# First pair of tile 1's heads scored in the mixer, and the expert stage's schedule moved up by one step

## What is computed

```
q      = x1 @ w_q                                # 8 heads x 2 halves x 128
scores = einsum('bshcd,hcnd->bshcn', q, sub_keys)
s1, i1 = top_k(scores[..., 0, :], 16); s2, i2 = top_k(scores[..., 1, :], 16)
cand   = s1[..., :, None] + s2[..., None, :]     # 256 sums
top_s, pos = top_k(cand, 16);  ids = expert numbers at pos;  gates = softmax(top_s)
act    = gelu(einsum('td,tkd->tk', x1, u_tab[ids])) * gates
out    = layer_norm(alpha * x1 + einsum('tk,tkd->td', act, v_tab[ids]))
```

## Time and profile before

| what | value |
|---|---|
| median of three runs | 3395.33 us |
| profiled run | 3388.38 us, span 3386.7 us |
| TensorE (PE) busy | 2825.3 us, 83% |
| VectorE (DVE) busy | 1882.9 us, 56% |
| ScalarE (ACT) busy | 604.3 us, 18% |
| GpSimd (POOL) busy | 1479.7 us, 44% |
| mean granted TensorE clock | 0.914 |
| moved by DMA | 981.57 MB, mean 290 GB/s |

### The profile page before, as it was taken

One profiled execution on the slowest core, in us unless ns is written; L12 is line 12 of the kernel. 1 busy time (PEld: TensorE's weight loads), 2 busy tenths in 40 slices (PEclk: granted clock), 3 DMA queues, 4 the chain that ended last, 5 costly groups with the idle time before them and its releaser, 6 DMA issues.

```text
span 3386.7 us, 32687 instructions
## 1 busy us (share of the span) xinstructions
PE 2825.3 (83%) x10195; PEld 1391.7 (41%) x10195; DVE 1882.9 (56%) x4610; ACT 604.3 (18%) x1334; POOL 1479.7 (44%) x1348
## 2 busy tenths in 40 slices
PE   8999978666345888748779999999999999999995
PEld 3455544433112455524334444444444444444341
DVE  2334434787579788768855556546656544444013
ACT  1321123222001788700000000000000000000000
POOL 0011001343544344344465666566665556664452
PEclk9999979877667899778889999999999999999998
DMA  3100021455588899898899999999999999998995
GB/s 105 50 25 25 25 73 66 140 168 172 192 303 291 322 387 379 321 386 334 308 385 388 404 399 404 373 396 399 404 404 374 370 396 406 392 396 341 364 329 195
DMA packets 307579, 981.57 MB, mean 290 GB/s; under 512 B 29905, under 2 KB 57681, under 8 KB 306641
## 3 DMA queue, kind: packets, MB, share of 16 engines
q0 software_dynamic: 184320, 671.17, 52.2%
q1 hardware_dynamic: 120464, 307.85, 24.1%
q10 hardware_dynamic: 2624, 0.46, 0.1%
HBM read 941.63 MB, written 37.75 MB: 289 GB/s over the span
## 4 chain that ended last, share of the span: by engine, by line
PE 27%; issue 13%; POOL 12%; DMA 11%; DVE 5%; ACT 2%; ACTq 1%; DVEq 1%; another core or an unknown queue 0%; POOLq 0%
DMA v_ring<-in_peer_v_dram,ids_t 10%; PE part L1720 8%; PE hid L1701 8%; POOL u_ring L1639 7%; PE acc L1758 6%; POOL v_ring L1653 5%; PE turn_ps L1693 4%; DVE u_ring L2009 2%; ACT dense_sums L1798 1%; PE part L1729 1%; DMA u_ring<-in_peer_u_dram,ids_u 1%; ACTq L1799 1%; ACT dense_sums L1800 1%; ACT room L1846 0%; PE sc_ps L1772 0%
## 5 line engine op out<-in xcount | busy, mean ns | idle before, releaser
L2009 DVE CUSTOM_DVE_ANT_0 u_ring<-u_ring,x_rows_in 128x1024 f32<-128x1024 f32 x560 | 676.1, 1224 | 505.4 <-DMA u_ring<-in_peer_u_dram,ids_u 460.4
L1653 POOL DMA_INDIRECT v_ring<-in_peer_v_dram,ids_t x600 | 634.5, 1057 | 543.0 <-PE acc L1758 373.9
L1639 POOL DMA_INDIRECT u_ring<-in_peer_u_dram,ids_u x560 | 622.4, 1112 | 488.0 <-DVE dots L2009 335.5
L1720 PE MATMUL part<-room 128*128 128x512 f32 x1536 | 693.8, 602 | 80.4 <-DVE room L1989 73.5
L1701 PE MATMUL hid<-x1t_dense,room 128*128 128x384 f32 x2048 | 702.7, 497 | 5.3 <-DMA room<-in_peer_ut_dram 3.8
L1701 PEld LDWEIGHTS hid<-x1t_dense,room 128*128 128x128 f32 x2048 | 387.4, 193 | 341.1 <-issue 103.9
L1720 PEld LDWEIGHTS part<-room 128*128 128x128 f32 x1536 | 292.1, 193 | 441.5 <-issue 336.7
L1758 PE MATMUL acc<-v_ring,line 128*32 128x512 f32 x2400 | 315.0, 645 | 86.3 <-DMA v_ring<-in_peer_v_dram,ids_t 81.9
L1836 ACT ACTIVATE room<-hid 128x384 f32<-128x384 f32 x128 | 62.8, 491 | 1476.7 <-PE hid L1701 1173.1
L1999 DVE TENSOR_TENSOR dense_sums<-dense_sums,part 128x512 f32<-128x512 f32 x186 | 125.5, 684 | 292.9 <-PE part L1720 256.0
L411 PE MATMUL bank<-w_ring,xt 128*128 128x512 f32 x512 | 225.1, 592 | 2.6 <-issue 2.6
(11 more groups left out here) (315 smaller groups left out, 2605.6 us busy)
## 6 DMA issues: line engine op xcount, KB each, us to landing
wq_pair<-in_peer_wq_dram SPq DMA_DIRECT2D x32, 2048.0 KB, 8.8
room<-in_peer_ut_dram SPq DMA_DIRECT2D x128, 512.0 KB
room<-in_peer_v_dram SPq DMA_DIRECT2D x128, 512.0 KB
gate_grid<-room SPq DMA_DIRECT2D x6, 4096.0 KB, 13.3
room<-gate_grid SPq DMA_DIRECT2D x32, 768.0 KB
w_ring<-in_w_in_dram SPq DMA_DIRECT2D x5, 2048.0 KB, 8.0
v_ring<-in_peer_v_dram,ids_t POOLq DMA_INDIRECT x600
u_ring<-in_peer_u_dram,ids_u POOLq DMA_INDIRECT x560
```

Of the source, the lines that this page charges most:

```text
L1639: pool.indirect_dma_start(u_ring[:, n % U_RING, :], None, peer_u, bass.IndirectOffsetOnAxis(ap=ids_u[:, q, k:k + 1], axis=0))\
L1653: pool.indirect_dma_start(row, None, peer_v, bass.IndirectOffsetOnAxis(ap=ids_t[:, q % 2, token:token + 1], axis=0))\
L1720: last = mm.matmul(part[k % 3][:], weights[:, n % 2, i, d * P:(d + 1) * P], vd[:, slot, half * 512:(half + 1) * 512], start=(i == 0), stop ...
L2009: vec.tensor_tensor_reduce(u_ring[:, n % U_RING, :], u_ring[:, n % U_RING, :], x1[:, q % 2, :], 1.0, 0.0, ALU.mult, ALU.add, dots[:, q % 2 ...
```

## The change

After tile 0's four pairs the mixer makes a fifth choice-like pass (`NEXT_TILE`, at n = 35): tile 1's x1 is read back from DRAM into `x1t_first`, pair 0's weights are loaded, TensorE makes the queries and scores of tile 1's first pair, and ScalarE copies them to `sc_pair`; VectorE doesn't choose them there. SP then loads pair 1's weights. The last tile's projection waits for that copy. `sc_pair` and `q_pair` lie in a new buffer `y_rows`, which both stages share (the scan's `ys` and `sq` and the expert stage's `y` lie in it too).

In the expert stage tile 1's pair 0 then belongs to step −1: VectorE chooses it in step 0 from `sc_pair`, and TensorE starts with pair 1. All tables but tile 0's own starts (`U_AT[0]`, `V_AT[0]`) move up by one step, and tile 0's 32 quads go through ten steps instead of eleven, the last three with four quads. `STEPS` falls by one.

```diff
-        ys = sb("ys", [P, SSD], to=scan)
-        sq = sb("sq", [P, SSD], to=scan)
+        ys, sq, sc_pair = y_rows[:, 0:SSD], y_rows[:, SSD:2 * SSD], y_rows[:, 0:2 * DKEY]
...
-        q_pair = sb("q_pair", [P, 2 * DKEY])
+        q_pair = y_rows[:, 2 * DKEY:4 * DKEY]
...
+        NEXT_TILE = HEADS // 2 + 1
+        CHOICES = (*range(HEADS // 2), NEXT_TILE)
...
-            return g if rest == 0 and 0 <= g < HEADS // 2 else None
+            return g if rest == 0 and g in CHOICES else None
...
+                    if t == NT - 1:
+                        sp.wait_ge(wq_free, 1).then_inc(wq_free, -1)
+                        load_pair(1)
...
                     if t == NT - 3:
                         sp.wait_ge(wq_free, 1).then_inc(wq_free, -1)
-                        sp.dma_start(wq_pair[:], peer_wq[:, 0:2 * DKEY].rearrange("(c p) n -> p c n", p=P)).then_inc(wq_in, 16)
-                        sp.dma_start(keys_pair[:], keys_t[:, 0:2 * DKEY]).then_inc(wq_in, 16)
+                        sp.dma_start(x1t_first[:].rearrange("p c n -> p (c n)"), x1t_dram[P:2 * P, :]).then_inc(wq_in, 16)
+                        load_pair(0)
...
-                        pe.wait_ge(wq_in, 32).then_inc(wq_in, -32)
+                        landed = 48 if choice(n, 0) == NEXT_TILE else 32
+                        pe.wait_ge(wq_in, landed).then_inc(wq_in, -landed)
...
-                        act.sem_inc(pair_for_dve, 2)
+                        if choice(n, 2) != NEXT_TILE:
+                            act.sem_inc(pair_for_dve, 2)
...
-                        if (g := choice(n, 5 + which)) is not None:
+                        if (g := choice(n, 5 + which)) is not None and g != NEXT_TILE:
...
-CHOSEN_AT = {1: 0, 2: 4, 3: 8, 4: 12, 5: 20, 6: 40, 7: 72}
+CHOSEN_AT = {1: -1, 2: 3, 3: 7, 4: 11, 5: 19, 6: 39, 7: 71}
...
-DENSE_AT = 18
+DENSE_AT = 17
...
-U_AT = (0, 17, 34, 67, 100)
+U_AT = (0, 16, 33, 66, 99)
...
-V_COUNTS = ((2,) + 10 * (3,), (2,) + 30 * (1,), (2,) + 30 * (1,), (2,) + 30 * (1,), 16 * (2,))
-V_AT = (6, 34, 67, 100, 133)
+V_COUNTS = ((2,) + 6 * (3,) + 3 * (4,), (2,) + 30 * (1,), (2,) + 30 * (1,), (2,) + 30 * (1,), 16 * (2,))
+V_AT = (6, 33, 66, 99, 132)
...
-NORM_AT = (26, 65, 98, 131, 149)
+NORM_AT = (25, 64, 97, 130, 148)
...
-                sp.wait_ge(q_done, n)
+                sp.wait_ge(q_done, n - 1)
...
-                sp.wait_ge(sc_done, n)
+                sp.wait_ge(sc_done, n - 1)
...
-                    dve.wait_ge(sc_done, n + 1)
-                    best_eight(vec, dve, b, sc_ps).then_inc(sc_seen, 1)
+                    if n:
+                        dve.wait_ge(sc_done, n)
+                    best_eight(vec, dve, b, sc_ps if n else sc_pair).then_inc(sc_seen, 1)
```

More of the change, by code:

```diff
@@ L123, in build_mixer @@
                 d_skip, ssd_norm_g, ln1_g, ln1_b, x1_dram, x1t_dram, peer_wq, keys_t, peer_u,
-                ids_first, top_first, dots_first, wq_pair, keys_pair, kept):
+                ids_first, top_first, dots_first, wq_pair, keys_pair, y_rows, kept):
     vec, act_, mm = nc.vector, nc.scalar, nc.tensor
@@ L730, in build_mixer @@
         x1_first = sb("x1_first", [P, D])
-        q_pair = sb("q_pair", [P, 2 * DKEY])
+        q_pair = y_rows[:, 2 * DKEY:4 * DKEY]
         qt_pair = sb("qt_pair", [P, 2 * DKEY])
-        sc_pair = sb("sc_pair", [P, 2 * DKEY])
         u_rows = sb("u_rows", [P, U_FIRST_RING, D])
@@ L1391, in normed_at, with build_experts @@
     return NORM_AT.index(step - lag) if step - lag in NORM_AT else None
-def build_experts(nc, x1_dram, x1t_dram, g_dram, ids_first, top_first, dots_first, wq, keys, peer_wq, keys_t, peer_u, peer_v, peer_ut,
+def build_experts(nc, x1_dram, x1t_dram, g_dram, ids_first, top_first, dots_first, wq, keys, y, peer_wq, keys_t, peer_u, peer_v, peer_ut,
                   ln2_g, ln2_b, out):
@@ L1415, in build_experts @@
         affine = sb("affine2", [P, 2, D])
-        y = sb("y", [P, D])
+        sc_pair = y[:, 0:4 * NKEYS]
         line = sb("line", [P, 2, (4 * LINE_QUADS + 1) * 32])
@@ L1766, in _ @@
                     pe.wait_ge(turn_read, turns)
-                    if n:
-                        pe.wait_ge(keys_in, n * 16)
-                    if n:
+                    if n > 1:
+                        pe.wait_ge(keys_in, (n - 1) * 16)
                         pe.wait_ge(sc_seen, n)
```

13 lines of the change are left out of this document (7 added, 6 removed).

## The result

The changed kernel takes 3414.59 us (median of four runs, 3412.46 to 3418.99) beside 3393.68 us for the kernel before on the same chip: ratio **1.0057, 95% interval 1.0034 to 1.0081**. That is slower by 19 to 21 us, outside the forecast range. The profiled execution is 24.0 us longer (3410.7 us against 3386.7 us).

The account below looks back on a forecast made before the run. It took VectorE to bound expert steps 0 to 5 and saw steps 6 to 16 within 3% of the full DMA rate; −9.5 + 1.3 + 6.7 + 3.1 = +1.6 us, median 3396.9 us, range 3382 to 3408.

Parts of the forecast that it names:

- Part 1: Expert stage's first steps: VectorE idle time falls in step 0 (−4.1) and step 6 (−5.4), −9.5 us, bounds −10.4 and −5.0.
- No whole step was won: Rival for the expert stage: step length not set by its work, so 24.4 us go, 3371; chance 0.05.
- Part 2: Expert stage, new step 6: the stall for the row products comes back one step on, +1.3 us, bounds 0 and 5.4.
- Part 4: Mixer's end: second weight load near 877 delays row gathers and the last projection's second half, +3.1 us, bounds 0 and 6.0.
- Part 5: Dense phase onward: everything moves by the same one step, order and content stay, 0 us, bounds −3 and +3.
- Part 3: New steps 13 to 15: a fourth quad each adds DMA bytes, +6.7 us, none from step 15, bounds 0 and 14.6.
- how near the limit is: Expert stage's DMA: query weights issued at 1214.94 are waited for 1.63 us at 1235.87, 21 us for 2 MB.
- the signs named: Checks: late last projection, step 0 some 27 us, steps 13 and 14 over 30 each, tile 4's first row at 1402.
- this stage runs within 3% of the rate of the stage that is full: Expert stage steps 6 to 16: DMA at 383 GB/s, share 1.00, against the dense phase's 393 at 1.01.
- The slower one: Rival, from new step 13: DMA has no reserve, each extra byte is paid, +12.4 us, median 3408; chance 0.16.
- The fourth quads are free: Rival, steps 13 to 15 and mixer: fourth quads and load cost nothing, −9.5 + 1.3, median 3387; chance 0.25.
- HBM limit of 358 GB/s: Steps 14 and 15 before, with the added quads: at this rate 71.8 us, +15.7; the forecast held the trace's 393 against it.

Follow-up runs that it names:

- e3: Kernel before with only the change's mixer part, its last load bringing pair 0's weights, expert stage as before; ratio to before 1.0006.
- e4: Changed kernel with the mixer's second load (pair 1's weights) issued behind the last tile's stores; ratio to the kernel before 1.0053.
- e9: Changed kernel with step 14's store and tile 5's first query weights with x1t (6.6 MB) held until 30 quads are used; ratio to before 1.0027.
- e11: Changed kernel with the edits of e10, e7 and e9 together; ratio to the kernel before 1.0008.
- e8: Changed kernel with the edits of e2 and e7 together; ratio to the kernel before 0.9989.
- e7: Changed kernel with the stage stores of steps 6, 8, 10 and 12 issued behind the next step's query weights; ratio to before 1.0035.
- e5: Changed kernel with the query weights of pairs 7 to 15 cut to one eighth, choices using stale weights; one run, 3399.29 us.
- e2: Changed kernel with tile 0's 48 rows in five steps and its quads in eleven steps from step 5; ratio to before 0.9990.
- e1: Changed kernel with the fourth quads undone (eleven quad steps) and tile 4's rows one step later; ratio to before 1.0044.
- e6: Changed kernel with the three four-quad steps put first (7 to 9) instead of 13 to 15; ratio to before 1.0027.
- e10: Changed kernel with the three four-quad steps in the middle (10 to 12); ratio to the kernel before 1.0066.
- e12: Changed kernel with the edits of e2 and e9, quads 2, 4, eight threes and two in the last step; ratio to before 0.9999.

## Why the prediction was wrong

*Part 1 (idle time removed, −9.5)* was right, and a little small. From the first query product to step 7's it is −10.6, which is parts 1 and 2 together (forecast −8.2). Step 0 takes 26.4 us (27 forecast). No whole step was won.

*Part 2 (+1.3)*: the step that waits for the row products (new step 6) is 31.2 us against 28.7 for the one that stood in its place, +2.5, inside its bounds. Parts 1 and 2 together are 2.4 us better than forecast.

*Part 4 (mixer, +3.1)* was right, and by the mechanism named. Around the mixer's last projection:

```profile
873.45 1.94 PE L966 MATMUL bank<-ident,x 128*128 128x128 f32 x8 [8.61 <-PEq L963]
877.19 2.05 PE L934 MATMUL bank<-keys_pair,qt_pair 128*128 128x128 f32 x8 [1.80 <-PEq L931]
...
882.85 9.95 PE L957 MATMUL bank<-w_ring,mix_t 128*128 128x512 f32 x16 [1.91 <-PEq L953]
...
894.75 1.23 DVE L1119 CUSTOM_DVE_ANT_0 u_rows<-u_rows,x_first 128x1024 f32<-128x1024 f32 x1 [3.32 <-DMA u_rows<-in_peer_u_dram,ids_first]
...
899.73 0.68 DVE L1084 SCALAR_TENSOR_TENSOR x<-x,bank 128x512 f32<-128x512 f32 x1
...
882.00:897.40 15.40, 9.95 (x16) 4.04 (x16) 6.92 (x11) 0.60 (x1) 6.84 (x6) 0.72 1.03 401
```

The score product (877.19) puts the first half off to 882.85, 9.4 us behind 873.45 (6.2 before, from 869.13 to 875.30), and this is covered. The second load runs under the row gathers at a share of 1.03 where 0.83 was the earlier trace rows, and VectorE waits 3.32 us for a row. From the store of the tile before (868.85 before, 873.16 after) to VectorE at the last projection it is 23.5 us before and 26.6 after: +3.1. e3 gives 2.3 to 2.4 at the stage's border, and e4, without the load there, has tile 7's rows 3.6 us sooner.

*Part 5 (0, bounds ±3)*: +3.0 from tile 4's row to the end, at the bound; over the twelve experiments this stretch is 1978.7 to 1995.3, so no cost is shown.

*Part 3 (fourth quads, +6.7, bounds 0 to 14.6)* is the term that was mis-sized: 15.6 us, a microsecond beyond the upper bound. The forecast put the 6.7 on steps 13 and 14 and nothing on step 15. Cut at the query product of step 13 and at VectorE's start on the last choice (1377.22 before, 1385.44 after), steps 13 and 14 cost 2.8 us (59.1 against 56.3) and step 15, up to tile 4's row, 12.8 (36.5 against 23.7). So the step that failed is the one that gave step 15 nothing, because its window before had a share of 0.81 and so 4.4 us free. That room was not where the gathers needed it. In the kernel before, the share is 0.95 from 1377 to 1392 and 0.54 only from there to 1400, when GpSimd's last refill was long out (1380.12) and it could issue nothing more until the last quad was used. After, both waits for V rows run at a full share (0.99 and 1.02, above), and during the first of them a 4 MB store is in flight that nobody needs yet (issued at 1382.43, landed 16.6 us later); e9 takes 7 us away with no byte less in the kernel. What the quads cost with stores and weights out of the way isn't isolated. In e11, steps 9 to the end of the interval cost 7.4 us more than before, but only 2.8 us more than in e8, which has the same order of stores and eleven steps of quads. The forecast of 6.7 lies in that range, and no run confirms it.

*What was missing altogether, +9.5 in steps 7 and 8.* Nothing in the prediction let a step cost more that gained no instruction. The diff moves the choices and with them the stage stores up by a step, but tile 0's quads still begin at step 6, and the next tile's x1 rows are loaded there. So store and x1 rows, which stood a step apart, now both precede the weights of one step. The prediction had the row (weights issued at 1214.94 and waited for 1.63 us) and read it as "how near the limit is" for part 3 only. It should have asked of each load on SP's queue what is ahead of it after the change. e7 (order alone), e5 (size alone) and e2 (store and rows a step apart) each remove the loss; e1, with neither, keeps 7.0 us of it.

Against the forecast of +1.6 the profiled +24.0 us is 22.4 us more: 9.5 from steps 7 and 8, 8.9 from part 3, 3.0 from part 5, 2.6 from the start of the stage and 0.8 from steps 9 to 12, less 2.4 from parts 1 and 2. Of the signs named, VectorE reached the last projection late (899.73) and step 13 took over 30 us, as forecast; step 14 took 28.3, and tile 4's first row left at 1421.94 instead of 1402.

*The reading "this stage runs within 3% of the rate of the stage that is full"* was wrong as a bound. With a seventh of the bytes out of steps 9 to 12 (324 GB/s instead of 379 in the two windows above) they take 28.2 us instead of 28.5. Yet where transfers pile up they land late, as the weights of step 7 and the V rows at the end did. So the reading was half of the truth: no bound on the mean, but no reserve where order or number changes.

*The rivals.* The slower one (DMA has no reserve, 3408) had the right sign and its point of decision occurred, TensorE waiting for V rows before L1763. Its price in the last steps, 14.6, is near the 15.6 measured. Its sum of +12.4 is still 11.6 us short, mostly for steps 7 and 8. "The fourth quads are free" is refuted by e6 and e11. Of the Trainium skill's page "DMA: Bandwidth & Descriptors", section "Where 436 GB/s comes from": by its HBM limit of 358 GB/s part 3 would be +15.7 (an estimate), and that this is near the measured 15.6 is chance. The same stretch runs at 386 to 407 GB/s in steps 13 and 14 in the rows above, at 420 and 405 during the two waits, and falls to 71 only behind them.

**What stays open.** A step in the middle with four quads reaches 38 to 39 us (step 11 in e10 and e11, in e11 with the stores behind the weights) by waits for V rows; why those rows come so late there, and not in the fours' other steps, wasn't taken apart. Nor were the x1 rows moved alone. Their 512 KB are 1.3 us at 402 GB/s (an estimate), while the weights' landing went from 21.6 us in e2 to 26.5, so the rest of that is not accounted for. What sets the pace of 28 us a step is open too. And no version is shown to be faster than the kernel before. e2 and e8 come nearest (0.9990 and 0.9989, each interval just holding 1); both beat the changed kernel by about 0.7%.

## What to carry to other kernels

In this kernel a DMA share of 1.00 went with transfers that came late when their order changed, and yet bytes didn't set the mean pace (e5). When a schedule is moved up, write down for each load which transfers stand ahead of it on its queue before and after, and price a load behind a large store by the trace's time from issue to landing, not by bytes. Cut a window with a share under 1 finer before calling the rest free: here the share was full during the waits and low only when no refill was left to issue. And ask which chain follows: here tile 4's first row waits for both the last quad and the last choice, which in the kernel before, e2 and e12 end within a microsecond of each other, so that speeding up one alone would win little there.
